# Expert choice of a mixture-of-experts layer in eight dependent VectorE steps, with three dummy products on TensorE and four weight units loaded earlier

## The reference

```python
    group_logits = jnp.einsum('td,dg->tg', h, w_group).astype(jnp.float32)
    g_sel = jnp.argmax(group_logits, axis=-1)
...
    expert_logits = jnp.einsum('td,de->te', h, w_router).astype(jnp.float32)
    expert_logits = expert_logits.reshape(T, N_GROUPS, EXPERTS_PER_GROUP)
    in_group = jnp.take_along_axis(expert_logits, g_sel[:, None, None], axis=1)[:, 0]
    in_prob = jax.nn.softmax(in_group, axis=-1)
    top_p, top_i = lax.top_k(in_prob, EXPERT_TOPK)
    top_p = top_p / jnp.sum(top_p, axis=-1, keepdims=True)
...
    for grp in range(N_GROUPS):
        hid = (jax.nn.silu(jnp.einsum('td,edf->tef', h, w_gate[grp]))
               * jnp.einsum('td,edf->tef', h, w_up[grp])) * combine[:, grp, :, None]
        y = y + jnp.einsum('tef,efd->td', hid, w_down[grp])
```

## Time and profile before

| | |
|---|---|
| runs shown, median (lowest to highest) | 795.76 us (793.94 to 797.08), 3 runs |
| the profiled execution, its own time | 796.86 us |
| its span | 795.1 us |
| PE busy | 742.2 us, 93% of the span |
| DVE, ACT, POOL busy | 443.9, 321.3, 44.0 us |
| DMA | 208.17 MB, mean 262 GB/s |
| TensorE's mean granted clock | 0.989 |

### The profile page before, as it was taken

One profiled execution on the slowest core, in us unless ns is written; L12 is line 12 of the kernel. 1 busy time (PEld: TensorE's weight loads), 2 busy tenths in 40 slices (PEclk: granted clock), 3 DMA queues, 4 the chain that ended last, 5 costly groups with the idle time before them and its releaser, 6 DMA issues. The chain is left out here.

```text
span 795.1 us, 13968 instructions
## 1 busy us (share of the span) xinstructions
PE 742.2 (93%) x5673; PEld 539.8 (68%) x5673; DVE 443.9 (56%) x772; ACT 321.3 (40%) x554; POOL 44.0 (6%) x39
## 2 busy tenths in 40 slices
PE   8999999899989999887876899999999999999998
PEld 5979976564646656544544587666548788888886
DVE  3899765544642331230330589688385865776665
ACT  4666433411432340340340664588432434343431
POOL 1000021001000000000000032301100000000000
PEclk9999999999999999998999999999999999999999
DMA  8894449988989999999999996610025445664201
GB/s 279 294 368 160 159 156 405 333 338 313 418 327 415 410 418 418 414 418 415 420 420 410 399 281 231 219 40 2 1 106 212 160 159 185 224 221 165 106 1 54
DMA packets 106387, 208.17 MB, mean 262 GB/s; under 512 B 7861, under 2 KB 55254, under 8 KB 98526
## 3 DMA queue, kind: packets, MB, share of 16 engines
q1 hardware_dynamic: 105406, 205.19, 68.8%
q10 hardware_dynamic: 864, 2.18, 0.8%
q0 software_dynamic: 64, 0.05, 0.0%
HBM read 206.31 MB, written 1.08 MB: 261 GB/s over the span
## 5 line engine op out<-in xcount | busy, mean ns | idle before, releaser
L2654 DVE TENSOR_TENSOR unit_parts<-ring,unit_parts 128x2048 fp32r<-128x2048 f32 x33 | 75.5, 2289 | 58.9 <-ACT unit_parts L1964 58.9
L1964 ACT ACTIVATE unit_parts<-ring 128x2048 fp32r<-128x2048 f32 x33 | 62.9, 1912 | 73.9 <-PE psa L1323 43.0
L1038 PE MATMUL psv<-ring,arena 128*32 128x256 f32 x960 | 60.9, 410 | 15.4 <-DMA ring<-in_w_up_dram 13.1
L1322 PE MATMUL psv<-column_parts,unit_parts 128*128 128x512 f32 (+1 forms) x192 | 65.5, 389 | 1.6 <-DVE arena L2742 1.4
L1322 PE MATMUL psa<-column_parts,unit_parts 128*128 128x512 f32 (+1 forms) x192 | 65.1, 388 | 0.0
L1038 PEld LDWEIGHTS psv<-ring,arena 128*32 128x32 f32 x960 | 34.2, 118 | 37.4 <-issue 22.6
L1323 PE MATMUL psv<-column_parts,unit_parts 128*128 128x256 f32 (+1 forms) x192 | 52.0, 271 | 0.0
L1323 PE MATMUL psa<-column_parts,unit_parts 128*128 128x256 f32 (+1 forms) x192 | 52.0, 271 | 0.0
L2785 POOL TENSOR_TENSOR small<-small,consts 128x2 f32<-128x2 f32 (+4 forms) x15 | 28.2, 1884 | 381.8 <-DVE small L2488 239.8
L1770 ACT ACTIVATE arena<-psv 128x256 f32<-128x256 f32 x8 | 3.1, 383 | 100.1 <-PE psv L1038 100.1
L1322 PEld LDWEIGHTS psv<-column_parts,unit_parts 128*128 128x128 f32 x192 | 36.1, 188 | 9.3 <-DVE unit_parts L2654 1.5
(11 more groups left out here) (441 smaller groups left out, 1688.7 us busy)
## 6 DMA issues: line engine op xcount, KB each, us to landing
ring<-in_w_gate_dram SPq DMA_DIRECT2D x43, 1024.0 KB, 9.3
ring<-in_w_up_dram SPq DMA_DIRECT2D x39, 1024.0 KB, 5.1
arena<-in_w_down_dram SPq DMA_DIRECT2D x32, 1024.0 KB
ring<-in_w_mod_dram SPq DMA_DIRECT2D x24, 1024.0 KB, 7.8
ring<-in_w_in_dram SPq DMA_DIRECT2D x23, 1024.0 KB, 10.0
ring<-in_w_down_dram SPq DMA_DIRECT2D x11, 1024.0 KB, 7.2
ring<-in_w_out_dram SPq DMA_DIRECT2D x8, 1024.0 KB, 8.0
arena<-in_w_in_dram SPq DMA_DIRECT2D x8, 512.0 KB, 16.3
```

Of the source, the lines that this page charges most:

```text
L1038: mm = pe.matmul(mG[32 * e:32 * e + 32, f0:f0 + FF], XT[:, k, 32 * e:32 * e + 32], w, start=(k == 0), stop=(k == KD - 1))
L1322: pe.matmul(both_parts(bank, t_0, t_1), hi, col_parts[:, :, k, t_0:t_1], start=(k == 0), stop=False)
L1964: act.activation(unit_parts[q % 3][:, 0, :], slot_of(NPRE + u_), ACT.Copy).then_inc(upper_done, 1)
L2654: vec.tensor_tensor(lo, slot_of(NPRE + at["mlp"] + 3 * n + kind), hi, ALU.subtract).then_inc(lower_done, 1)
```

## The change

Three edits.

1. The chain of the choice. The logits of the chosen group are no longer picked out and summed: `(gw - gmw) + logit` leaves the chosen group's 32-column row part as it is and pushes the others far down, since `tie_g` now holds multiples of `BIG`. The eight largest of the 32 are taken by one instruction for each block (`max`), two of them are copied into `wanted`, `match_replace` writes a marker over these two, and `sel` is where the marked copy differs. The softmax weights are built from comparisons with the largest logit. Two small fills of constants (`memset`) are new ahead of the output sums.
2. `keep_busy` runs 3 dummy products in place of 12 ahead of the wait for `chosen_done`.
3. SP issues expert units 0 to 3 (the gates of the first pass, into the ring) ahead of its wait for `delta_out_done` and of units 8 and 11 and the context weights `cw_ka`, and no longer behind them.

```diff
-    put("tie", np.tile(np.concatenate([np.arange(NG, 0, -1), np.arange(EG, 0, -1)])[None], (P, 1)))
+    put("tie", np.tile(BIG * np.arange(NG, 0, -1)[None], (P, 1)))
...
-            keep_busy(PSX[0], 12)
+            keep_busy(PSX[0], 3)
...
             stream(NPRE - 4, NPRE)
+            def ring_place_free(n):
+                sp.wait_ge(*freed[NPRE - NS + n])
+            for n in range(4):
+                ring_place_free(n)
+                load_expert_unit(sp, n, 0)
             sp.wait_ge(delta_out_done, 1)
             load_expert_unit(sp, 8, 0)
             load_expert_unit(sp, 11, 0)
...
-            for n in range(4):
-                ring_place_free(n)
-                load_expert_unit(sp, n, 0)
             sp.wait_ge(v_ready, at["delta"])
...
+            vec.memset(inside[:, :, NE:], -3.0 * BIG * NG)
+            vec.memset(wanted[:, :, 2:8], -3.0 * BIG * NG)
...
             link(vec.tensor_reduce(gmw, gw[:], AX, ALU.max))
-            vec.tensor_tensor(goh[:], gw[:], over(gmw, NG), ALU.is_equal)
-            for b in range(NB):
-                ins = vec.scalar_tensor_tensor(picked[:, b], gw[:, b].unsqueeze(2).broadcast_to((P, NG, EG)), gmw[:, b:b + 1],
-                                               el[:, b], ALU.is_equal, ALU.mult)
-            link(ins)
-            link(vec.tensor_reduce(ing[:], picked.rearrange("p b g e -> p b e g"), AX, ALU.add))
-            link(vec.tensor_reduce(im, ing[:], AX, ALU.max))
...
-            vec.tensor_tensor(sel[:], g4, s8.unsqueeze(2).broadcast_to((P, NB, NG, EG)), ALU.mult).then_inc(chosen_done, 1)
+            for b in range(NB):
+                ins = vec.scalar_tensor_tensor(inside[:, b, 0:NE].rearrange("p (g e) -> p g e", g=NG),
+                                               gw[:, b].unsqueeze(2).broadcast_to((P, NG, EG)), gmw[:, b:b + 1],
+                                               el[:, b], ALU.subtract, ALU.add)
+            link(ins)
+            for b in range(NB):
+                ins = vec.max(best8[:, b], inside[:, b, 0:NE])
+            link(ins)
+            link(vec.tensor_copy(wanted[:, :, 0:2], best8[:, :, 0:2]))
+            for b in range(NB):
+                ins = vec.match_replace(left[:, b], wanted[:, b], inside[:, b], -4.0 * BIG * NG)
+            link(ins)
+            vec.tensor_tensor(sel[:], left[:, :, 0:NE], inside[:, :, 0:NE], ALU.not_equal).then_inc(chosen_done, 1)
...
-            link(vec.tensor_tensor(oh2[:], s8[:], oh1[:], ALU.subtract))
-            link(vec.tensor_tensor(wi[:], oh1[:], over(f1, EG), ALU.mult))
-            link(vec.tensor_tensor(oh2[:], oh2[:], over(f2, EG), ALU.mult))
-            link(vec.tensor_tensor(wi[:], wi[:], oh2[:], ALU.add))
-            link(vec.tensor_tensor(comb[:], g4, wi.unsqueeze(2).broadcast_to((P, NB, NG, EG)), ALU.mult))
+            for b in range(NB):
+                vec.tensor_scalar(comb[:, b], inside[:, b, 0:NE], best8[:, b, 0:1], f1[:, b:b + 1], ALU.is_equal, ALU.mult)
+                ins = vec.tensor_scalar(second[:, b], inside[:, b, 0:NE], best8[:, b, 0:1], f2[:, b:b + 1], ALU.is_lt, ALU.mult)
+            link(ins)
+            link(vec.tensor_tensor(comb[:], comb[:], second[:], ALU.add))
+            link(vec.tensor_tensor(comb[:], comb[:], sel[:], ALU.mult))
```

More of the change, by code:

```diff
@@ L2294, in gain_rows @@
                                          every(ffn_bc[:, half * 512:half * 512 + 512], KD), ALU.mult)
+            inside, left = (rt[:, a:a + NB * (NE + 6)].rearrange("p (b n) -> p b n", b=NB) for a in (512, 640))
+            best8, wanted = (rt[:, a:a + NB * 8].rearrange("p (b n) -> p b n", b=NB) for a in (592, 608))
+            vec.memset(inside[:, :, NE:], -3.0 * BIG * NG)
+            vec.memset(wanted[:, :, 2:8], -3.0 * BIG * NG)
             for m in range(2 * NB):
@@ L2323, in f @@
                 return v_.rearrange(f"p ({' '.join(nm)}) -> p {' '.join(nm)}", **dict(zip(nm[1:], d[1:])))
[L2325 to L2333, removed]
+            sel, ex = f(0, NB, NE), f(136, NB, NG + 1)
+            gm, gw, gmw = f(160, NB), f(162, NB, NG), f(170, NB)
+            gsum, second = f(180, NB), f(192, NB, NE)
+            f1, f2, comb = f(346, NB), f(348, NB), f(382, NB, NE)
             pos, cmax = f(446, NB, NE), f(510, 1)
-            tie_g, tie_e = c("tie")[:, 0:NG], c("tie")[:, NG:NG + EG]
+            tie_g = c("tie")
             logits = PSX[1][:, 0:NB * NR].rearrange("p (b n) -> p b n", b=NB)
@@ L2344, in _ @@
             link(vec.tensor_reduce(gmw, gw[:], AX, ALU.max))
-            vec.tensor_tensor(goh[:], gw[:], over(gmw, NG), ALU.is_equal)
             for b in range(NB):
-                ins = vec.scalar_tensor_tensor(picked[:, b], gw[:, b].unsqueeze(2).broadcast_to((P, NG, EG)), gmw[:, b:b + 1],
-                                               el[:, b], ALU.is_equal, ALU.mult)
+                ins = vec.scalar_tensor_tensor(inside[:, b, 0:NE].rearrange("p (g e) -> p g e", g=NG),
+                                               gw[:, b].unsqueeze(2).broadcast_to((P, NG, EG)), gmw[:, b:b + 1],
+                                               el[:, b], ALU.subtract, ALU.add)
             link(ins)
-            link(vec.tensor_reduce(ing[:], picked.rearrange("p b g e -> p b e g"), AX, ALU.add))
-            link(vec.tensor_reduce(im, ing[:], AX, ALU.max))
             for b in range(NB):
-                ins = vec.scalar_tensor_tensor(w1[:, b], ing[:, b], im[:, b:b + 1], tie_e, ALU.is_equal, ALU.mult)
+                ins = vec.max(best8[:, b], inside[:, b, 0:NE])
             link(ins)
[L2355 to L2358, removed]
+            link(vec.tensor_copy(wanted[:, :, 0:2], best8[:, :, 0:2]))
             for b in range(NB):
-                ins = vec.scalar_tensor_tensor(w2[:, b], rem[:, b], m2[:, b:b + 1], tie_e, ALU.is_equal, ALU.mult)
+                ins = vec.match_replace(left[:, b], wanted[:, b], inside[:, b], -4.0 * BIG * NG)
             link(ins)
-            link(vec.tensor_reduce(wm2, w2[:], AX, ALU.max))
-            for b in range(NB):
-                ins = vec.scalar_tensor_tensor(s8[:, b], w2[:, b], wm2[:, b:b + 1], oh1[:, b], ALU.is_equal, ALU.add)
-            link(ins)
-            g4 = goh.unsqueeze(3).broadcast_to((P, NB, NG, EG))
-            vec.tensor_tensor(sel[:], g4, s8.unsqueeze(2).broadcast_to((P, NB, NG, EG)), ALU.mult).then_inc(chosen_done, 1)
+            vec.tensor_tensor(sel[:], left[:, :, 0:NE], inside[:, :, 0:NE], ALU.not_equal).then_inc(chosen_done, 1)
             dve.wait_ge(power_done, ROUTE_POWER)
@@ L2371, in _ @@
                                          rstd[:, b:b + 1].broadcast_to((P, NG)), ALU.subtract, ALU.mult)
-            link(vec.tensor_tensor(m2, m2, im, ALU.subtract))
-            vec.tensor_tensor(ex[:, :, NG], m2, rstd, ALU.mult).then_inc(route_exp_req, 1)
+            link(vec.tensor_tensor(f2, best8[:, :, 1], best8[:, :, 0], ALU.subtract))
+            vec.tensor_tensor(ex[:, :, NG], f2, rstd, ALU.mult).then_inc(route_exp_req, 1)
             bank = v_take()
-            self_ = sel.rearrange("p b g e -> p b (g e)")
             dve.wait_ge(chosen_done, 1)
-            link(vec.scalar_tensor_tensor(pos[:], bank[:, 0:2 * NE].rearrange("p (b e) -> p b e", b=NB), 1.0, self_,
+            link(vec.scalar_tensor_tensor(pos[:], bank[:, 0:2 * NE].rearrange("p (b e) -> p b e", b=NB), 1.0, sel[:],
                                           ALU.add, ALU.mult))
@@ L2397, in _ @@
             link(vec.reciprocal(f1, f1))
-            vec.tensor_tensor(f2, ex[:, :, NG], f1, ALU.mult)
-            link(vec.tensor_tensor(oh2[:], s8[:], oh1[:], ALU.subtract))
-            link(vec.tensor_tensor(wi[:], oh1[:], over(f1, EG), ALU.mult))
-            link(vec.tensor_tensor(oh2[:], oh2[:], over(f2, EG), ALU.mult))
-            link(vec.tensor_tensor(wi[:], wi[:], oh2[:], ALU.add))
-            link(vec.tensor_tensor(comb[:], g4, wi.unsqueeze(2).broadcast_to((P, NB, NG, EG)), ALU.mult))
-            combs = comb.rearrange("p b g e -> p b (g e)")
+            link(vec.tensor_tensor(f2, ex[:, :, NG], f1, ALU.mult))
+            for b in range(NB):
[4 more added lines that the diff above has]
+            link(vec.tensor_tensor(comb[:], comb[:], sel[:], ALU.mult))
+            combs = comb
             mG, mHT, mSc = PSV[1], PSV[2], (PSX[1], PSV[0])
```

2 lines of the change are left out of this document (removed).

## The result

| | runs | median (lowest to highest) | ratio to before [95% interval] |
|---|---|---|---|
| before | 4 | 795.27 us (793.94 to 797.08) | |
| after | 4 | 802.73 us (801.96 to 803.63) | 1.0093 [1.0069, 1.0116] |

The changed kernel is 7.5 us slower, outside the range that I gave and on the other side. The profiled execution took 802.83 us, its span is 801.0 us.

What follows compares the result with a forecast made beforehand. TensorE's queue was taken to bound the kernel up to the first expert pass, the weight stream from 227.5 to 430 us. A gain of 3.2 us from the median 795.76 gave 792.5 us, range 790.6 to 795.0.

Steps and rivals of the forecast that it cites:

- Sum: Whole kernel: a gain of 3.2 us, taken at L987, brings the median of 795.76 to 792.5 us.
- signs of being wrong: MATCH_REPLACE or MAX over 0.5 us, first-pass L1038 over 4, TensorE waits at L911 or first ups, stretch not 203 us.
- The choice: VectorE's chain to `sel`: MAX pair 0.40 us, MATCH_REPLACE pair 0.60, ending at 213.64 us in place of 215.20.
- Rival (a): In the choice, MAX or MATCH_REPLACE takes 0.5 us and more each: time 793.6 to 794.8 us; chance 0.13.
- my dear case: In the choice, four match-and-replace instructions at 0.2 us each make the pair 0.8 and the gain 3.0 us.
- The dummies: TensorE ahead of L987: three products end at 213.1 us; by itself L987 could start 1.7 us earlier.
- Rival (b): TensorE's clock falls at the routing through idle time: 794.2 us, or 800.0 if both groups are slowed; chance 0.08.
- The gates ahead: SP's queue: gates issued at 170.5 and 174.2 us spare a wait for first-pass ups until 225; worth nothing alone.
- `w_out` and L911: Early gates sharing the DMA engines could make `w_out` land 3.4 us later, costing TensorE 1.5 us at L911.
- The forecast for the stream: Weight stream: pause begins near 218 us, next gates at 223.1, last wait for ups ends at 426.6, stretch 203 us.
- (d): End of the stream: the last pass's up half avoids the low clock, giving 790.8 us; chance 0.18.
- (c): The stream does not start earlier, since the gates ahead do not empty the queue: 793.5 us; chance 0.06.

Runs made afterwards that it cites:

- e3: Kernel before with an unused SBUF tile of eight columns behind the constants, all later tiles 32 bytes further on: 806.21 us, ratio 1.0114.
- e2: Changed kernel with an unused SBUF tile of eight columns behind the constants, so SBUF addresses as before: 794.17 us, ratio 0.9973.
- e12: All three edits with addresses kept, the kernel of e2 measured again in more rounds: 793.21 us, ratio 0.9960 to the kernel before.
- e4: Kernel before with all tiles behind the constants 64 bytes further on: 806.32 us, ratio 1.0119.
- e9: Kernel before with 3 dummy products in place of 12, addresses as before: 796.07 us, ratio 0.9997.
- e10: Kernel before with only the four gate units moved ahead in SP's queue, addresses as before: 796.54 us, ratio 1.0003.
- e11: Changed kernel with addresses as before and the gate units back at their old place in SP's queue: 797.38 us, ratio 1.0010.
- e1: Changed kernel with eight unused columns put back into the constants input, SBUF addresses as before: 794.31 us, ratio 0.9979.

## Why the prediction was wrong

**The step that failed** is the list on which the *Sum* rests, not a term in it. I costed the choice, the dummies, the fills and the gates ahead, and read the line of the diff on `tie` only as new values for the chain. That it also made the constants eight columns narrower, and with them moved every tile behind, had no term. In its place the runs show 9 to 10.6 us: e3 has it alone (1.0114, 9.1 us), and e2 and e12, one kernel, take it away alone (from 1.0093 to 0.9973 and 0.9960, 9.6 and 10.6 us). My 792.5 and these make 801.6 to 803.1, and 802.73 was measured. Nor did a rival hold it. My 0.05 for slower by over 0.5% was for the clock, "or something unseen". One of my signs of being wrong did come, a stretch from the first gates to the last ups that is not 203 us long, and I had no term that could have made it so.

What the loss consists of, in the profiled execution of the changed kernel: the stream from SP's gates to the last ups takes 212.6 us instead of 203.6, so 9.0 us, and 2.3 us are lost ahead of the routing, less 3.6 us won. That makes 7.7 us at the last wait for ups. The spans differ by 5.9, because what follows took 363.4 us instead of 365.3; over the profiled executions of all the kernels it took 362.0 to 366.9, so I read nothing into it. Ahead of the routing 1.5 us of delay are there by 152 us. With the tiles off in the kernel before (e3, e4) it is 0.9, with the addresses kept 0 to 0.8, so that the slower loads make all of the 1.5 is not shown. 0.58 us are the wait for `w_out` at L911.

**The choice**: right, and a little better than taken. The MAX pair took 0.29 us (I took 0.40), the two match-and-replace with their loads 215.01 to 215.43, 0.42 (I took 0.60). Rival (a) did not happen. That a match-and-replace is two instructions, as the Trainium skill lists it (VectorE: DVE Perf Modes, "Two Vector instructions with no wait between them"), the rows show; but a load of the values takes 0.09 us and a replacement 0.18, where my dear case had 0.2 for each of the four.

**The dummies**: right with the short choice. L605 has 6 records and takes 1.48 us (I had 1.34), TensorE idles 0.21 and 0.49 us (I had 0.7 and 0.5), and L1012 takes 3.81 us as before. Rival (b) names a real mechanism: with the long choice (e9) the idle time is 2.04 us and the clock falls. So the dummies that I called an overhang were also what kept the clock up, and fewer of them did not pay with the long choice. The shorter choice alone was not run.

**The gates ahead**: right. Nothing alone (e10); without them TensorE waits for the first ups (e11). I had the wait ending at 225; it ends at 227.1 in an execution 1.6 us late. What I had not worked out is what the wait costs. In my expectation of e11 it has its 2 us, but I let the stream start and run on as if TensorE had not waited, and gave e11 a gain of 2.5 to 3 us. The trace shows the stretch longer by 4.7 us instead.

**`w_out` and L911**: the wait that I had named as a danger of the gates ahead came, and not from them. With the gates ahead and the addresses kept (e1, e2, e10, e12) there is none; with the gates at their old place and the tiles off it is 0.48 us (e3) and 0.71 (e4). The 0.58 us in the changed kernel come with the slower transfers.

**The forecast for the stream**: with addresses kept most times that I had named came within 0.5 us in e12: L987 213.85 (213.8), L1012 215.64 (215.6), the gates at 170.95 and 223.10 (170.5 and 223.1), the last wait for ups ending at 426.70 (426.6), the stretch 203.6 us (203). The pause began near 220 instead of 218, and the second pair of gates was issued at 174.7, not 174.2. Some of the agreement is luck: this execution is 0.4 us later than that of the kernel before at the first L911, and the way from L605 to L987 was 0.4 us shorter than I took it. The last half ran at low clock as before, so (d) did not happen, and (c) did not either.

**What stays open**: why the packets lose what they lose. I had thought that a piece that begins off a multiple of 256 costs one step of 256 bytes more: 33 steps for 32 in a piece of 8 KB, 9 for 8 in one of 2 KB, 3 for 2 in one of 512 bytes, so 3%, 12% and 50%. The packets of e3 are 2.3%, 4.6% and 12% longer. Short ones do lose relatively more, but the sizes are not those. And a packet's own place does not tell it alone: those of 8 KB, which all go into the ring, take 1.0 ns more with the ring off, 1.9 with only the arena off, and 7.2 with both.

## What to carry to other kernels

Read each line of a diff for what it does to the layout too. A constant that gets narrower in the first tile moves all others, and the sign of it here is a DMA rate that is lower at about the same share, also in stretches that the edit does not touch: compare such a stretch first. Keep the places that DMAs write to on multiples of 256 bytes. And an edit worth nothing alone can be what lets two others pay: the dummies (e9), the gates ahead (e10), and the choice with the dummies (e11) each measure nothing, the three together 3.3 us in e12 and 2.1 in e2.

## What the runs showed of the hardware

- A tile's place in SBUF sets how fast DMAs write to it: 416 GB/s from 228 to 430 us on multiples of 256 bytes, 398, 398 and 394 at 32, 64 and 128 bytes off, 415 again when moved by 256. The Trainium skill (DMA: Bandwidth & Descriptors, "How a descriptor splits into AXI transactions") says that a transaction has to start from an address aligned to 256 bytes, and tells it of reads. The runs agree on the 256, for the side that is written. By the beats that the page counts a start further off would cost more; the runs show 32, 64 and 128 bytes costing the same within their intervals, and the measurement decides.
- What it costs a packet, with all tiles 32 bytes off (e3, 228 to 430 us): 310.9 to 318.1 ns for 8 KB, 84.2 to 88.1 for 2 KB, 27.0 to 30.2 for 512 bytes.
- Behind 2.04 us of idle TensorE, some products and 0.49 us more the granted clock was 0.50 (e9), and low about 1 us after a wait of 2.89 us had ended (e11). Behind 0.21 and 0.49 us it stayed at 1.00 (e12), and so it did behind a wait of 3.03 us, so the length of the wait alone does not tell.
- MAX over 32 columns takes about 0.15 us for each of a pair, MATCH_VALUE_LOAD 0.09 and MATCH_REPLACE over 38 columns 0.18 us.
